# Decoder layer: first modulation and first seven projection units in slices of 256 features, index dots within the first value unit, squares of four units summed at once

## What is computed

```python
mod = silu(c) @ w_ada + b_ada                 # c: 1024 -> 6 vectors of 1024
shift1, scale1, gate1, shift2, scale2, gate2 = split(mod, 6)
h = rms_norm(x, norm1_g) * (1 + scale1) + shift1
q, k, v, qi, ki, wi, u_pool, g_attn, g_pool = split(h @ w_in)
q, k = rms_norm(q per head of 64), rms_norm(k per head of 64)
iscore = sum_h relu(qi_h @ ki.T) * wi_h       # 4 index heads, causal
sel = top 128 keys of each query by iscore    # SEQ // 4
attn = softmax(q @ k.T / 8 - slope * distance, over sel) @ v     # 8 heads
y_pool = (trailing mean of u_pool over 2, 4, 8, 16 tokens - token) @ w_grp * pool_scale @ w_pool_br
merged = sigmoid(g_attn) * (attn @ w_attn_br) + sigmoid(g_pool) * y_pool
x = x + gate1 * (merged @ w_out)
h2 = rms_norm(x, norm2_g) * (1 + scale2) + shift2
up = depthwise causal conv of width 3 over (h2 @ w_up), plus bias   # 2 x 2816
x = x + gate2 * ((silu(up_a) * up_b) @ w_down)
```

## Time and profile before

| | us |
|---|---|
| median of 3 runs | 754.72 |
| the profiled execution, device time | 759.15 |
| its span, first to last instruction | 757.2 |
| TensorE busy | 739.7 (98%) |
| VectorE busy | 379.0 (50%) |
| ScalarE busy | 306.6 (40%) |
| GpSimd busy | 312.3 (41%) |

### The profile page before, as it was taken

How to read it: one execution, slowest core, us unless ns; L and a number is a source line. 1 busy time by engine, 2 the same in 40 slices (tenths; PEclk the granted TensorE clock), 3 DMA queues, 4 the chain that set the end, 5 groups by cost and what they waited for, 6 DMA issues and landing times.

```text
span 757.2 us, 9497 instructions
## 1 busy us (share of the span) xinstructions
PE 739.7 (98%) x3568; PEld 597.2 (79%) x3568; DVE 379.0 (50%) x693; ACT 306.6 (40%) x501; POOL 312.3 (41%) x165
## 2 busy tenths in 40 slices
PE   4989999999999999999999999999999999999997
PEld 3467788888777777887899888888788888888886
DVE  2588699972446551774685435464443433004002
ACT  4224513256756763334455343434334343212120
POOL 1125338562623332547423444444444444443431
PEclk9969989999999999999999999999999999999999
DMA  8995511221113113644338344323323321233301
GB/s 327 381 338 204 187 55 57 71 97 56 57 57 112 57 56 107 262 159 128 97 95 267 112 111 112 91 76 112 101 68 110 111 99 68 84 112 112 137 2 56
DMA packets 83995, 92.75 MB, mean 122 GB/s; under 512 B 2035, under 2 KB 66287, under 8 KB 83951
## 3 DMA queue, kind: packets, MB, share of 16 engines
q1 hardware_dynamic: 82719, 87.43, 35.6%
q10 hardware_dynamic: 1232, 4.72, 1.7%
HBM read 90.05 MB, written 2.10 MB: 122 GB/s over the span
## 4 chain that ended last, share of the span: by engine, by line
PE 96%; DVE 1%; DMA 1%; ACT 1%; SPq 0%; issue 0%; DVEq 0%; ACTq 0%
PE bank L1471 42%; PE bank L1491 21%; PE bank L1480 21%; PE bank L1547 2%; PE bank L1741 1%; PE bank L1719 1%; PE bank L1707 1%; PE bank L1513 1%; PE bank L1625 1%; DMA xtok<-in_x_dram 1%; PE bank L1565 1%; PE bank L1614 1%; ACT junk L747 1%; PE bank L1518 1%; PE bank L1775 1%; PE bank L1532 0%
## 5 line engine op out<-in xcount | busy, mean ns | idle before, releaser
L650 POOL TENSOR_TENSOR wsplit<-stage,wsplit 128x1024 fp32r<-128x1024 f32 (+1 forms) x120 | 275.0, 2295 | 395.2 <-ACT wsplit L732 391.7
L1471 PE MATMUL bank<-hT,wsplit 128*128 128x512 f32 (+1 forms) x1264 | 295.3, 386 | 0.0
L1471 PEld LDWEIGHTS bank<-hT,wsplit 128*128 128x128 f32 x1264 | 231.8, 190 | 46.5 <-issue 0.9
L732 ACT ACTIVATE wsplit<-stage 128x1024 fp32r<-128x1024 f32 (+1 forms) x120 | 119.8, 1000 | 280.9 <-PE bank L1480 196.7
L1480 PE MATMUL bank<-hT,wsplit 128*128 128x512 f32 (+1 forms) x632 | 152.8, 384 | 0.0
L1480 PEld LDWEIGHTS bank<-hT,wsplit 128*128 128x128 f32 x632 | 114.7, 188 | 23.5 <-issue 0.8
L1491 PE MATMUL bank<-wsplit,guT 128*128 128x512 f32 x528 | 119.8, 389 | 0.0
L1491 PEld LDWEIGHTS bank<-wsplit,guT 128*128 128x128 f32 x528 | 99.1, 188 | 20.5
L1429 DVE SCALAR_TENSOR_TENSOR yb<-bank,conv,yb 128x511 f32<-128x511 f32 (+1 forms) x44 | 32.9, 749 | 65.1 <-ACT yb L1022 64.3
L1429 DVE SCALAR_TENSOR_TENSOR ya<-bank,conv,ya 128x511 f32<-128x511 f32 (+1 forms) x44 | 33.0, 749 | 59.2 <-ACT ya L1022 58.4
L1364 DVE TENSOR_TENSOR tmp_last<-bank,gate_row 128x512 f32<-128x512 f32 x8 | 5.5, 688 | 101.7 <-PE bank L1491 101.7
(11 more groups left out here) (188 smaller groups left out, 731.8 us busy)
## 6 DMA issues: line engine op xcount, KB each, us to landing
stage<-in_w_up_dram SPq DMA_DIRECT2D x44, 512.0 KB, 5.2
stage<-in_w_in_dram SPq DMA_DIRECT2D x17, 1024.0 KB, 5.3
stage<-in_w_down_dram SPq DMA_DIRECT2D x10, 1024.0 KB, 5.0
ada_early<-in_w_ada_dram SPq DMA_DIRECT2D x8, 1024.0 KB, 10.1
ada<-in_w_ada_dram SPq DMA_DIRECT2D x7, 1024.0 KB, 11.7
ada_mid<-in_w_ada_dram ACTq DMA_DIRECT2D x4, 1024.0 KB, 8.1
stage<-in_w_out_dram SPq DMA_DIRECT2D x4, 1024.0 KB, 6.1
ada_last<-in_w_ada_dram SPq DMA_DIRECT2D x4, 1024.0 KB, 11.1
```

What stands on the lines that cost most here:

```text
L650: pool.tensor_tensor(unit_split(n, 1), unit_source(n), unit_split(n, 0).bitcast(F32), ALU.subtract).then_inc(low, 1)
L732: me.did(act.activation(unit_split(n, 0), unit_source(n), ACT.Copy), high)
L1471: pe.matmul(out_bank[:, tokens], hi[:, k, :], rhs[:, part, k, tokens], start=k == 0 and part == 0, stop=False)
```

## The change

**Slices.** `x` is normed by token before it is turned: ScalarE squares and roots each tile as it lands, VectorE scales it (`xn`), TensorE turns all 8 blocks into 8 banks. The weights of vectors 0 and 1 are loaded as four slices of 256 features of each vector (`load_first`), with all 1024 inputs. TensorE makes the sums of a slice (`first_sums`): eight calls with a weight `cpad` of 32 columns (column 0 is silu of c, the rest zero), 512 moving columns (256 of each vector), each writing one of four groups of 32 output partitions. ScalarE copies the bank, four column turns (`first_columns`) sum over the groups, and two blocks of `hT` follow, now by one scaling with gain and shift (`full1`).

**Seven units together.** The weights of the first seven units (index queries, `kw`, four of q; 896 columns) are loaded and split by input block, not by unit: eight units of one block of 896 columns. For each block TensorE runs 21 matmuls into seven banks; the sums of the next slice stand behind the even blocks and its columns within the odd ones. VectorE makes the low parts of these eight.

**Order.** The small loads stand behind x and before all else, c is loaded on ScalarE's queue. The value units come before those of u. All index dots stand within the first value unit and the start of the second. Squares of four units are kept, summed at once by four calls to four groups of partitions (`squares`, with `halves` as a weight of 32 columns), copied and turned (`squares_turn`). Vector 3 is loaded by rows during the slices and summed in the third and fourth of them. Vector 4 is summed after the last merged unit, through `ada_mid`, and turned after the first tile of the output projection's second half.

The core of the diff (indentation inside the engines' programs cut by two levels):

```diff
-ROW_TURN = {1: 0, 3: 1, 4: 2, 2: 3, 5: 4}
+ROW_TURN = {3: 0, 2: 1, 4: 2, 5: 3}
+COLUMN_TURN = {3: 0, 4: 1}
+FIRST = (("qi", 0), ("qi", 1), ("kw", 0), ("q", 0), ("q", 1), ("q", 2), ("q", 3))
+FIRST_AT = (512, 640, 768, 0, 128, 256, 384)
+FIRST_BANK = (3, 4, 0, 1, 2, 5, 6)
+FIRST_COLUMNS = ((C_Q, 512, 0), (C_QI, 384, 512))
+KS = 896
+KQ = KD // 2
...
+    def first(self):
+        for q in range(KQ):
+            self.items.append(("first", "in", (C_Q, C_QI), 2 * q, 2 * q + 2, 1))
+            self.last_use.append(None)
+            for r in range(2):
+                self.units.append((1, r, KS))
+                self.house()
+                self.item_of.append(q)
+                self.last_use[q] = ("unit", len(self.units))
+        for at, name in enumerate(FIRST):
+            self.opens(name, "dve", FIRST_BANK[at])
+        self.ring = NBANK - 1
...
-    for kind, n in (("qi", 2), ("kw", 1), ("q", KA), ("u", KA), ("v", KA)):
+    s.first()
+    for kind, n in (("v", KA), ("u", KA)):
...
+        if kind == "first":
+            for c0, wide, c in FIRST_COLUMNS:
+                sp.dma_start(slot[:, 0:2 * KS].rearrange("p (k n) -> p k n", n=KS)[:, :, c:c + wide],
+                             weights[w][:, k0:k1, c0:c0 + wide]).then_inc(stage_in[n % NSTAGE], 16)
+            return
...
+    def load_first(q):
+        for half in range(2):
+            ks = slice(half * KQ, (half + 1) * KQ)
+            for j in range(2):
+                c0 = j * D + 2 * q * P
+                sp.dma_start(ada_first[q][:, ks, 2 * j * P:2 * (j + 1) * P], ada[:, ks, c0:c0 + 2 * P]
+                             ).then_inc(ada_in[q][half], 16)
...
+    def load_row(k):
+        if k % 4 == 0:
+            sp.wait_ge(sums_ok, k // 4 + 1)
+        sp.dma_start(ada_row[k][:, :], ada[:, k, 3 * D:4 * D]).then_inc(ada_row_in[k], 16)
...
+        if n == KQ + 4:
+            sp.wait_ge(sums_ok, KQ - 1)
+            sp.dma_start(wgrp[:, :, :], w_pool_grp[0].rearrange("g c d -> c g d")).then_inc(wgrp_in, 16)
...
+        act.wait_ge(x_in[t], 16)
         me.did(act.activation(junk[:, t % 2, :], xtok[:, t, :], ACT.Square,
                               accum_out=tstat[:, 0, t:t + 1]), x_sum)
...
+        me.settle()
+        me.did(act.activation(tstat[:, 2, t:t + 1], tstat[:, 0, t:t + 1], ACT.Sqrt, bias=eps[:, 0:1],
+                              scale=1.0 / D), root_ok)
+    act.wait_ge(x_t, NT)
+    for k in range(0, KD, 2):
+        me.did(act.activation(xT[:, k, :], banks[k][:, :], ACT.Copy), x_kept[0])
...
+    def squared(part, m, name):
+        if part and not m:
+            act.wait_ge(sq_used, 1)
+        me.did(act.activation(sq[part][m][:, :], bank(name)[:, :], ACT.Square), sq_ok)
+    def square_rows(part):
+        act.wait_ge(sq_used, part + 1)
+        if part:
+            act.wait_ge(sq_t, part)
+        me.did(act.activation(sqrow[:, :], SUMS[part][0][:, :], ACT.Copy), sq_row)
...
+    act.wait_ge(mod_sum, KD)
+    query(0)
+    query(1)
+    relus(2)
+    high_parts(KD + 2)
+    relus(6)
+    high_parts(KD + 3)
+    relus(8)
+    query(2)
+    relus(10)
     v_raw(0)
+    relus(12)
+    query(3)
     v_raw(1)
+    square_rows(0)
     v_kept(0)
...
+        j, q = (2, 4)[n // 4], n % 4
+        act.dma_start(ada_mid[n % 2][:, :, :], ada[:, 2 * q:2 * q + 2, j * D:(j + 1) * D]
                       ).then_inc(ada_mid_in[n % 2], 16)
...
+    load_mid(4)
+    load_mid(5)
     high_parts(sch.unit["out", 1, NT - 1] + 1)
+    load_mid(6)
+    load_mid(7)
     def square_half(half, t):
...
+    def first_vectors(q):
+        ks, rows_at = slice(2 * q, 2 * q + 2), slice(KD + 2 * q, KD + 2 * q + 2)
+        dve.wait_ge(col_ok, q + 1)
+        me.did(dve.tensor_tensor(mod[:, ks], OB[:, MC:MC + 2], vec[:, V_ADA + 2 * q:V_ADA + 2 * q + 2],
+                                 ALU.add))
+        me.did(dve.tensor_tensor(mod[:, rows_at], OB[:, MC + 2:MC + 4],
+                                 vec[:, V_ADA + KD + 2 * q:V_ADA + KD + 2 * q + 2], ALU.add), first_mod)
         me.settle()
...
+        me.did(dve.scalar_tensor_tensor(out=gs[:, 0, ks], in0=mod[:, rows_at], scalar=1.0,
+                                        in1=vec[:, V_NORM1 + 2 * q:V_NORM1 + 2 * q + 2],
+                                        op0=ALU.add, op1=ALU.mult))
         me.settle()
...
+    def first_low(k):
+        dve.wait_ge(h_hi, k + 1)
+        me.did(dve.tensor_tensor(hT[:, 1, k, :], full1[:, k % 2, :], hT[:, 0, k, :].bitcast(F32),
+                                 ALU.subtract), h_lo)
+    dve.wait_ge(c_silu, 1)
+    dve.wait_ge(consts, 13)
+    me.did(copy_of(cpad[:, :, 0], csil[:, :]), c_pad)
+    me.did(dve.reciprocal(invn[:, :], invn[:, :]))
+    for t in range(NT):
+        dve.wait_ge(root_ok, t + 1)
+        me.did(dve.reciprocal(tstat[:, 3, t:t + 1], tstat[:, 2, t:t + 1]))
+        me.settle()
+        me.did(dve.tensor_scalar(xn[:, t, :], xtok[:, t, :], tstat[:, 3, t:t + 1], None, ALU.mult), xn_ok)
+    dve.wait_ge(x_t, NT)
+    for k in (KD - 1, 1, 3, 5):
+        me.did(copy_of(xT[:, k, :], banks[k][:, :]), x_kept[1])
...
+    for q in range(KQ):
+        first_vectors(q)
+        for k in (2 * q, 2 * q + 1):
+            if k % 2 == 0:
+                dve.wait_ge(x_kept[0], k // 2 + 1)
             if k >= 2:
                 dve.wait_ge(h_lo, k - 1)
...
+            me.did(dve.tensor_scalar(full1[:, k % 2, :], xT[:, k, :], gs[:, 0, k:k + 1], mod[:, k:k + 1],
+                                     ALU.mult, ALU.add), n_ok)
+        for k in (2 * q, 2 * q + 1):
+            first_low(k)
+            low_parts(k + 1)
+        for k in ((), (), (0, 1, 2, 3, 4), (5, 6, 7))[q]:
+            mod_row_of(3, k)
...
+    top_rounds(8)
     pool_mean(0)
+    top_rounds(2)
+    pool_mean(1)
     mod_vector(3)
     top_rounds(2)
-    pool_mean(1)
-    mod_vector(4)
+    pool_mean(2)
+    top_rounds(1)
+    mixed(0)
+    pool_mean(3)
     top_rounds(2)
...
+    for q in range(KD // 2):
+        mod_rows(4, q)
     gate_vector(0)
...
+        if t == 1:
+            mod_vector(4)
+            me.settle()
...
+    def first_sums(q):
+        if q == 0:
+            pe.wait_ge(c_pad, 1)
+            pe.wait_ge(x_kept[1], 1)
+        else:
+            pe.wait_ge(first_mod, q)
+        for half in range(2):
+            pe.wait_ge(ada_in[q][half], 32)
+            for g in range(KQ):
+                k = half * KQ + g
+                mm = pe.matmul(OB[32 * g:32 * (g + 1), :], cpad[:, k, :], ada_first[q][:, k, :],
+                               start=half == 0, stop=half == 1)
+        mm.then_inc(sums_ok, 1)
+    def first_columns(q):
+        pe.wait_ge(row_ok, q + 1)
+        for n in range(4):
+            mm = pe.matmul(OB[:, MC + n:MC + n + 1], rowsum[:, n * P:(n + 1) * P], ones[:, 0:1],
                            start=True, stop=True)
-        mm.then_inc(mod_turn, 1)
+        mm.then_inc(col_ok, 1)
+    def first_products(k, made, part, a, names=FIRST, start=False, stop=False):
+        pe.wait_ge(made, k + 1)
+        pe.wait_ge((high, low)[a], k + 1)
+        for name in names:
+            at = FIRST_AT[FIRST.index(name)]
+            mm = pe.matmul(bank(name)[:, :], unit_split(k, a)[:, 0, at:at + P], hT[:, part, k, :],
+                           start=start, stop=stop)
+        return mm
+    pe.wait_ge(rows_in, 16 * ROW_LOADS)
+    pe.wait_ge(x_kept[0], 1)
+    pe.transpose(banks[0][:, 0:V_END], rows[0:V_END, 0, :], ident[0:V_END, 0:V_END])
+    pe.transpose(banks[0][:, P:2 * P], rows[:, 1, :], ident[:, :])
+    left = (TAPS + 1) * 2 * KF - P
+    pe.transpose(banks[0][:, 2 * P:2 * P + left], rows[0:left, 2, :], ident[0:left, 0:left]).then_inc(rows_t, 1)
+    first_sums(0)
+    first_columns(0)
+    pe.wait_ge(vecs, 1)
+    for n in range(2):
+        pe.wait_ge(x_kept[n], KD // 2)
+    for k in range(KD - 1):
+        first_products(k, h_hi, 0, 0, start=k == 0)
+        if k % 2:
+            first_columns(k // 2 + 1)
+        first_products(k, h_lo, 1, 0)
+        first_products(k, h_hi, 0, 1).then_inc(used, 1)
+        if k % 2 == 0 and k < KD - 2:
+            first_sums(k // 2 + 1)
...
+    def squares(part):
+        pe.wait_ge(sq_ok, KA * (part + 1))
+        if part:
+            pe.wait_ge(i_relu, IH * (NT - 1))
+        else:
             pe.wait_ge(wi_ok, 1)
+        for g in range(KA):
+            mm = pe.matmul(SUMS[part][0][32 * g:32 * (g + 1), :], halves[:, :], sq[part][g][:, :],
+                           start=True, stop=True)
+        mm.then_inc(sq_used, 1)
+    def squares_turn(part):
+        pe.wait_ge(sq_row, part + 1)
         for t in range(NT):
...
+    index_dots(0)
+    await_bank(pe, ("v", 0))
+    value_high(0, 0, 3)
+    index_dots(2)
+    value_high(0, 3, 6)
+    index_dots(4)
+    value_high(0, 6, 8)
+    value_low(0, 0, 2)
+    index_dots(6)
+    value_low(0, 2, 5)
+    index_dots(8)
+    value_low(0, 5, 8)
+    await_bank(pe, ("v", 1))
+    value_high(1, 0, 1)
+    index_dots(10)
+    value_high(1, 1, 8)
```

(18 more changed lines are left out.)

485 lines of the change are left out of this document (186 added, 299 removed).

## The result

The changed kernel takes 766.82 us (median of 4 runs, 764.54 to 768.09), the kernel before 755.05 beside it: a ratio of 1.015, interval 1.012 to 1.0179. It is slower by 11.8 us where 12.3 us of gain were forecast. Its profiled execution took 767.63 us, with a span of 765.7.

A forecast was written before the change was run, and what follows sets the result against it. TensorE, busy 739.7 of 757.2 us, was taken as the bound, saving only where it idles, runs at half clock or does other work. -19.9 + 1.1 + 1 + 4 + 1.5 = -12.3 us gave 742.4 us on the median, range 732 to 753.

The forecast's parts named there:

- 7 x 24 = 168 matmuls at 0.227 make 38.1 us, as before: Seven units together: their matmuls keep the old pitch of 0.227 us each, 38.1 us in all.
- the slower case: Rival, sums and square sums: column groups of 32 don't run side by side, 6.9 us a slice, 765 us; chance 0.06.
- Part 1, the start: Head of the kernel: first product at 23 us instead of 40.98, bounds 20.5 and 26.
- Part 2: Seven units with three more slices, 8.8 us, and 3 us lost at half clock: done at 72.9, gain 19.9.
- Two wide only: Rival, slices and square sums: packed column groups run only in pairs, +7 us, 749.4; chance 0.19.
- rival of slow slices: Start: slices of 1 KB rows arrive slower than TensorE eats them, some 8 us later, 750 us; chance 0.05.
- Part 3: After the seven units: index dots, squares and turns +1.1 us; selection, first round taken 15 us behind, +1 us.
- Selection late: Rival, after the seven units: index scores take 27.5 us again, TensorE waits 9.7 us instead of 1, 751 us; chance 0.10.
- Part 4: Output projection with vector 4's sums and turn: 4 us of issue, landing and waits, 1.5 of half clock.
- Carrying the sum to the median: The -12.3 us, made inside the profiled execution of 759.15 us, was applied to the median of 754.72: 742.4.

The follow-up runs named there:

- samedist: The changed kernel with `halves` placed ahead of xtok and a filler of its old size in its place, restoring all old distances: 752.64 us, ratio 0.9951.
- before_shifted: The kernel before, with 96 idle bytes behind `halves` and nothing of the change: 771.77 us, ratio 1.0209.
- aligned: The changed kernel with 32 idle bytes behind `halves`, so hT is at a multiple of 64 bytes again: 766.67 us, ratio 1.013.
- late_turn: early_loads with the turn of vector 4 one token tile later and the first turn of x2 behind it: 748.86 us, ratio 0.9909.
- early_loads: samedist with vector 4's first two loads ahead of the merge's last chunks, the other two behind only part of the high parts: 748.24 us, ratio 0.9885.

## Why the prediction was wrong

**The step that failed** is "7 x 24 = 168 matmuls at 0.227 make 38.1 us, as before", and with it every product behind them, which the sum left out as unchanged. `halves` was counted as an operand of the square sums and never as 120 more bytes in front of hT. This is 15 us: samedist differs from the changed kernel in addresses alone and is at 0.9951 against 1.015. Shown by before_shifted too, where the shift without the change costs 2.1%. Neither the sum nor a rival held anything of it; the slower case, column groups that don't run side by side, came near the measured time (765) by a cause that did not occur. Without this step the forecast would still have been too good: samedist gained 3.7 us where 12.3 were forecast, and parts 3 and 4 and the last paragraph say why.

**Part 1, the start:** 20.32 us, just outside the lower bound of 20.5, where 23 was taken.

**Part 2:** a slice of sums 1.85 us where 2.0 was taken, so four column groups do run side by side: 6.9 us one after another, 3.7 times as fast. "Two wide only" and "not side by side" are out. Half clock was 3.4 us long (6.8 in aligned and late_turn), the 3 us of loss too many. The 6 us after which the clock came back before were misread too: from the first product at 40.98 to beyond 48 us, where 0.64 was granted, it is some 8. Seven units done at 70.07 against 72.9, even at the slower pitch. The rival of slow slices did not occur.

**Part 3:** the first round of selection came 17.9 us behind the seven units (87.98 less 70.07) where I took 15. That is 11.3 us later than before, nearly all of the 11.9 us of slack, and TensorE waited 1.76 us for a pooled mix at 147.84. The half clock behind it cost as much again (5.55 against 3.79); samedist waited 1.87 us in the same place and no half clock followed. "Selection late" was right in kind, at 1.8 to 3.5 us of its 9.7. In samedist the gate sums are 20.4 us early; the forecast there was 19.6 (19.9 less 1.1 less 1, and 1.8 for vector 4's turn, which leaves this part).

**Part 4:** 7.3 us were forecast (4 + 1.5, and the turn's 1.8), 14.0 came in samedist. Two terms were mis-sized. The row sums stood at 1.28 us; four of the eight ran beside GpSimd's subtractions at 2.3 and 3.3, so the eight took 17.5 instead of 9.7, which pushed out the release of the buffers and so the last two loads. The earlier trace rows had the warning: a maximum of 2131 against a median of 1285, which I read as spread. And the half clock cost 4.4 us (1.74 on the turn, 2.70 on the tile), not 1.5. The landings themselves were near the forecast (5.1 to 9.1 us in the kernel after, 5.1 to 9.4 in samedist, 5.4 to 10.5 forecast). early_loads mends the timing of the loads and gets back 6.7 us in the trace, 4.4 in the medians.

**Carrying the sum to the median.** In the profiles samedist is 6.3 us faster, by the medians of the ratio 3.7. The profiled execution before was 4.4 us over its median, and I subtracted from it as though the excess lay elsewhere. Up to the MLP's first product it had it all: behind that, both take 368 us. The excess goes with the granted clock. The later executions of the kernel before took 753.75 to 754.95 us at a mean clock of 0.992 or 0.993, and the profiled one had 0.986. By an estimate from these means it ran 9 us longer at half clock, which loses 4.5. The half clock at 102 us, from which part 3 took 2.9 us of gain, is probably part of that: before_shifted, profiled at a mean of 0.991, has 1.00 granted from 98 to 106 us. The kernel before was profiled only once, so this isn't shown. The account of samedist against the forecast then closes: 12.3 less 3.7 is 8.6, of which part 4 is 6.7, the carrying 2.6, and the earlier gate sums give back 0.8.

## What to carry to other kernels

When a diff grows or shrinks any resident tile, write down the addresses of the large matmul operands before and after: here the pitch is lowest when the moving operand lies a multiple of 256 bytes from the stationary one, and 96 bytes of idle space decide more than the whole change. Keep it so by placing new constants behind or ahead of all of these operands. Compare the mean granted clock of the executions too, before a stretch at half clock is booked as a gain. A long VectorE operation with its operands in SBUF must be priced beside what GpSimd does in the same microseconds; a maximum far over the median in a group is where to look. A wait for the slowest chain can't be moved away by reordering TensorE: find what ends last (here the gate and the norm), and feed that earlier.

## What the hardware showed that I had not expected

- The pitch of back-to-back 512-column matmuls in the split format, with no other engine at work: 226.7 to 227.7 ns at a distance of 0 modulo 256 bytes, 229.1 at 64, 232.4 to 234.2 elsewhere, in steps of 32; wherever the pair lay, to 1 ns.
- VectorE and GpSimd took turns by whole instructions when VectorE's operands were in SBUF: 8 columns took 2.3 us, 1024 took 3.38 (1.28 alone), and GpSimd's 2.34 became 3.07. With an operand in a bank VectorE kept its 0.68 and GpSimd its 2.35.
- Four column groups of 32 with 512 moving columns: 16 instructions in 1.85 us, where 24 with one column took 10.4.
